# A hybrid decoder step on one core: attention output built transposed, experts drained behind their loop, pairs of expert rows added on TensorE

## The chip, the core and the metric

The kernel runs on one core of a Trainium2 chip. The metric is the device time of one execution in microseconds (us). Matrix products run on TensorE (PE; PEld is its weight load), elementwise work on VectorE (DVE), ScalarE (ACT) and GpSimd (POOL). SP issues most transfers; ACT and POOL issue some. Engines meet at counting semaphores: `.then_inc(s, 1)` counts up, `wait_ge(s, n)` holds the engine's queue until the count is there. Each engine works through its own list in order.

## The reference, cut to what matters

2048 prompt tokens and 8 x 4 sample tokens (2080 rows of 1024) go through one layer.

```python
u, v_a, q, k, v_b, gates = split(h @ w_in)            # h = modulated rms_norm(x)
out_a = gelu(u) * (tril(w_s) @ layer_norm(gelu(v_a)) + b_s)   # chunks of 128 tokens, 4 groups
p = sink_softmax(rope(q) @ rope(k).T)                 # 8 heads of 64, 2 key/value heads, window 128
out_b = p @ v_b
x1 = x + gate1 * ((g_a * (out_a @ w_pa) + g_b * (out_b @ w_pb)) @ w_o)
# each row of h2 goes to 2 of 32 experts, in blocks of 128 rows of one expert
yb = (silu(xb @ w_gate[e]) * (xb @ w_up[e])) @ w_down[e]
y  = rms_norm(x1 + gate2 * (weight_0 * yb_0 + weight_1 * yb_1)) * normf_g
```

Everything is f32. Most large products are made of three products of a high and a low part in fp32r (`three`, L254); the others are plain f32 products.

## The kernel before, in words

Six stages follow each other, each with its own block of engine programs and a barrier of all engines between: `condition`, `sweep_mixers` (to about 620 us), `sweep_gate_a`, `sweep_gate_b` with the router, `list_blocks` and `experts` (about 1558 to 2146 us), `combine` (to the end).

**sweep_mixers** goes over 16 tiles of 128 tokens and one of 32 (the sample). The attention's second half runs one tile late. On PE, `tile(i)` (L856) runs: q projection, k and v projection, the 16 transposes of the probabilities of tile i-1 (after `probs`, ACT's last exponential), v projection of mixer A, the products of probabilities and values of tile i-1 (L887: 16 of 128 x 64, into rows of tokens), transposes of q and k, two of eight steps of the u projection, four transposes of `out_b`, the other six steps, the spatial mixing (L918). Then follow the transposes of the next h, the scores (L928) and the transposes of `out_a`. DVE's `tile` (L753) runs: rotary of q, `sums` (L727, the reciprocal 1/z), rotary of k, `back_probs` (L738: half of the turned probabilities out of PSUM; ACT copies the other half), `norm_v` with `out_b` in its midst (L744: the result times 1/z, out of PSUM), `low_b`, the norm of the next tile, `out_a`, `low`, softmax. The output of the attention is kept as high and low parts of its transpose (`obT`) and stored for the next stage.

**sweep_gate_a** starts by loading and splitting 16 slices of 128 weight rows (w_in's gate, w_pa, w_pb) through four buffers.

**list_blocks** works out which block of 128 rows belongs to which expert and stores the fields of each block, with the ring slot of the expert's weights, and the number of blocks.

**experts** has a ring of four weight slots, filled by SP. Step b does, on PE: transposes of hidden rows b-1, gate and up products of block b, transposes of gathered rows b+1, down products of b-1 (L2081). ACT's step (L1969): hidden rows b-1, tanh of b, high part of the gathered rows b+1, high part of the weights of b+2 (L1942, two halves), the weighing of the output of b-1 (L1958), records. POOL's step: gather b+2, scatter b-1 (L1883). The loops run steps in pairs up to the next even number at or above the number of blocks, so that step b makes the output of block b-1.

**combine** goes over the 17 tiles again: DVE adds the two expert rows of each token (L2206), multiplies by gate 2 (L2208), adds x1 (L2211) and, after ACT's sum of squares and POOL's root, scales to the final norm (L2215). Pairs are loaded by ACT's queue (L2174), x1 and the gates by SP's, four tiles ahead. DVE starts after all three gate rows have landed.

## Time and profile before

| | us |
|---|---|
| median of 3 runs (2252.49 to 2255.87) | 2255.22 |
| the profiled execution | 2261.7 |
| its span, first to last instruction | 2260.1 |
| PE busy | 1931.8 (85%) |
| DVE busy | 1094.1 (48%) |
| ACT busy | 759.3 (34%) |
| POOL busy | 269.8 (12%) |

A busy time is a sum over the whole span, and the stages have different limits; so a stretch says more than the sum. In a timeline each row gives start and duration, the engine, the line, the operation with output and inputs, how many instructions were merged (x8), and in brackets how long the engine was idle before it and which work ended that. A plain f32 product shows as two PE records, a transpose as one. The granted clock of TensorE is 1.00 at 2.4 GHz and 0.50 at 1.2 GHz.

### The profile page before, as it was taken

To read this page: it belongs to the slowest core of one execution; us is meant where nothing else is said; L and a number is where in the kernel's file an instruction comes from. 1 tells how busy PE (TensorE), PEld (TensorE's weight loads), DVE (VectorE), ACT (ScalarE), POOL (GpSimd) and SP (SyncE) were. 2 spreads that over 40 slices of the span, in tenths; PEclk is the share of its full clock that TensorE was granted. 3 is DMA by queue.
4 is the path that set the end of the run, shared out by engine and by line. 5 is a ranking of instruction groups with operands and counts; after the bars stand their busy time and mean duration, and the time that the engine had idled before them with its cause. 6 is when DMAs were issued, how large, how long until landed. Compare 5 with 4: busy or idle time off the path is not lost. (4 is left out here: it accounts for less than half of the span.)

```text
span 2260.1 us, 30494 instructions
## 1 busy us (share of the span) xinstructions
PE 1931.8 (85%) x9577; PEld 1502.8 (66%) x9578; DVE 1094.1 (48%) x1912; ACT 759.3 (34%) x1323; POOL 269.8 (12%) x334
## 2 busy tenths in 40 slices
PE   6699999999869999996599999991799999999600
PEld 2588888888647777773488888860566666666400
DVE  3466666666330000012355555553566666666558
ACT  2244444444130000002212112110466666666512
POOL 0000000000000000000000101001122222222213
PEclk9799999999779999998799999995799999999855
DMA  8321222222084454534544433412987454999187
GB/s 282 122 87 74 87 86 95 95 94 78 22 307 182 178 193 166 205 112 171 180 149 148 149 130 139 145 63 62 320 299 263 162 192 141 310 306 307 35 334 290
DMA packets 196410, 381.98 MB, mean 169 GB/s; under 512 B 46174, under 2 KB 125534, under 8 KB 190178
## 3 DMA queue, kind: packets, MB, share of 16 engines
q1 hardware_dynamic: 156532, 304.92, 38.9%
q0 software_dynamic: 21936, 59.40, 7.0%
q10 hardware_dynamic: 17904, 17.19, 2.5%
q8 instruction: 20, 0.33, 0.1%
q14 instruction: 18, 0.15, 0.0%
HBM read 297.10 MB, written 104.26 MB: 178 GB/s over the span
## 5 line engine op out<-in xcount | busy, mean ns | idle before, releaser
L2011 DVE TENSOR_TENSOR gate_up_lo<-expert_ring,gate_up_hi 128x2048 fp32r<-128x2048 f32 x106 | 238.2, 2289 | 162.3 <-ACT gate_up_hi L1942 162.3
L1942 ACT CAST gate_up_hi<-expert_ring 128x2048 fp32r x106 | 196.6, 1902 | 159.8 <-issue 122.0
L260 PE MATMUL mix<-w_mix_hi,hT_hi 128*128 128x512 f32 (+3 forms) x544 | 203.8, 375 | 3.8 <-DVE hT_lo L640 2.6
L262 PE MATMUL mix<-w_mix_lo,hT_hi 128*128 128x512 f32 (+3 forms) x544 | 198.7, 365 | 0.0
L261 PE MATMUL mix<-w_mix_hi,hT_lo 128*128 128x512 f32 (+3 forms) x544 | 198.4, 365 | 0.0
L2081 PE MATMUL ex<-expert_ring,hidden_T 128*128 x400 | 181.8, 597 | 8.8 <-issue 8.6
L1150 DVE SCALAR_TENSOR_TENSOR ma_rows<-tanh_rows,ga 128x512 f32<-128x512 f32 (+1 forms) x34 | 21.8, 683 | 340.5 <-PE ga L262 190.1
L260 PE MATMUL ex<-gate_up_hi,gathered_T_hi 128*128 128x512 f32 x408 | 165.4, 405 | 6.1 <-DVE gathered_T_lo L2002 6.1
L262 PE MATMUL ex<-gate_up_lo,gathered_T_hi 128*128 128x512 f32 x408 | 161.0, 394 | 0.0
L261 PE MATMUL ex<-gate_up_hi,gathered_T_lo 128*128 128x512 f32 x408 | 160.5, 393 | 0.0
L260 PE MATMUL gb<-w_b_hi,h_parts_b 128*128 128x512 f32 (+1 forms) x272 | 109.7, 403 | 28.7 <-DVE w_b_lo L1449 18.9
L2081 PEld LDWEIGHTS ex<-expert_ring,hidden_T 128*128 128x128 f32 x400 | 72.0, 190 | 84.9 <-issue 84.8
L1883 POOL DMA_INDIRECT weighted_rows<-y_block,row_records x50 | 81.9, 1638 | 382.4 <-ACT y_block L1958 382.4
L260 PE MATMUL ga<-w_a_hi,h_parts 128*128 128x512 f32 (+1 forms) x272 | 110.0, 404 | 19.2 <-DVE w_a_lo L1135 14.4
L260 PEld LDWEIGHTS mix<-w_mix_hi,hT_hi 128*128 128x128 f32 (+1 forms) x544 | 100.7, 185 | 23.8 <-issue 7.3
L262 PEld LDWEIGHTS mix<-w_mix_lo,hT_hi 128*128 128x128 f32 (+1 forms) x544 | 100.5, 185 | 18.5
L261 PEld LDWEIGHTS mix<-w_mix_hi,hT_lo 128*128 128x128 f32 (+1 forms) x544 | 100.8, 185 | 16.5
L260 PE MATMUL ga<-w_a_hi,mixer_parts 128*128 128x512 f32 (+1 forms) x272 | 106.3, 391 | 3.0 <-DVE w_a_lo L1135 2.9
L260 PE MATMUL gb<-w_b_hi,merged_T_hi 128*128 128x512 f32 (+1 forms) x272 | 107.5, 395 | 1.1 <-ACT merged_T_hi L1397 1.1
L261 PE MATMUL ga<-w_a_hi,h_parts 128*128 128x512 f32 (+1 forms) x272 | 107.9, 397 | 0.0
L261 PE MATMUL gb<-w_b_hi,h_parts_b 128*128 128x512 f32 (+1 forms) x272 | 107.7, 396 | 0.0
L262 PE MATMUL ga<-w_a_lo,h_parts 128*128 128x512 f32 (+1 forms) x272 | 107.6, 396 | 0.0
(295 smaller groups left out, 3813.4 us busy)
## 6 DMA issues: line engine op xcount, KB each, us to landing
expert_ring<-in_w_gate SPq DMA_DIRECT2D x32, 1024.0 KB, 6.1
expert_ring<-in_w_up SPq DMA_DIRECT2D x32, 1024.0 KB, 8.6
expert_ring<-in_w_down SPq DMA_DIRECT2D x32, 1024.0 KB, 10.3
h_parts<-hT_split SPq DMA_DIRECT2D x16, 1024.0 KB
mixer_parts<-oT_split SPq DMA_DIRECT2D x32, 512.0 KB
w_ada_part<-in_w_ada SPq DMA_DIRECT2D x16, 1024.0 KB, 10.7
h_parts_b<-hT_split SPq DMA_DIRECT2D x16, 1024.0 KB
expert_pairs<-weighted_rows ACTq DMA_DIRECT2D x16, 1024.0 KB, 8.0
```

Source lines behind the costliest of these rows:

```text
L260: nc_mm(out, left[0], right[0], start=first, stop=False)
L261: nc_mm(out, left[1], right[0], start=False, stop=False)
L262: return nc_mm(out, left[0], right[1], start=False, stop=last)
L1150: last = nc.vector.scalar_tensor_tensor(out=ma[0:m, par, at], in0=tg[0:m, at], scalar=1.0, in1=ps[2 + n][0:m, :], op0=ALU.add, op1=ALU.mult)
L1883: pool.indirect_dma_start(out=s["y2"], out_offset=bass.IndirectOffsetOnAxis(ap=rec[:, slot, 0:1].bitcast(U32), axis=0), in_=y[:, slot % 2, ...
L1942: nc.scalar.copy(wg[par][0][:, n * HG:(n + 1) * HG], w[:, bass.ds(slot * GU + n * HG, HG)]).then_inc(w_hi, 1)
L2011: nc.vector.tensor_tensor(wg[par][1][:, at], w[:, bass.ds(slot * GU + n * HG, HG)], wg[par][0][:, at].bitcast(F32), ALU.subtract).then_inc ...
L2081: last = nc.tensor.matmul(ps[5 + n][:, :], hT[par][:, k, :], w[:, bass.ds(at, 512)], start=(k == 0), stop=(k == 1))
```

## The change

It has six parts.

1. In the mixers the probabilities are multiplied by 1/z before they are turned (`weighed`); values are the stationary operand and four heads' turned probabilities the moving one, so that four products give the transposed output at once, one key/value head in each half of the partitions. The four transposes of `out_b` go. PE turns the probabilities behind the v projection and makes the products amid the u projection; DVE copies its half of them inside `norm_v`, and norms the next tile before `low_b`; on ACT the gelu of v goes ahead of the copy of probabilities, and `keep_v` goes behind `back_out`.
2. The output's rows now stand in another order, so `w_pb` is loaded in that order, each slice in two transfers of 64 rows.
3. `list_blocks` stores a fifth field, half of the number of blocks less one; two more small DVE steps.
4. The experts' loops end one step earlier; the last block's down product, weighing and scatter come behind the loop, with a record slot of their own. ACT weighs between the two halves of the weights' cast.
5. SP loads x1 of tiles 0 to 7 and the three gate rows into ring slots 0, 2 and 1 once their last expert's weights are split. The ring is kept for `combine`.
6. In `combine` PE adds the two expert rows by products with the identity into PSUM, and DVE multiplies by the gate from there. Its loops are written out.

```diff
+                nc.vector.tensor_tensor(sc[:, :, :], sc[:, :, :], tiny[:, 48:56].unsqueeze(2).to_broadcast([P, NH, 2 * P]),
+                                        ALU.mult).then_inc(weighed, 1)
...
-            def out_b(i):
-                dve.wait_ge(pv_done, i + 1)
-                nc.vector.tensor_tensor(ob[:, :].rearrange("p (h d) -> p h d", d=HD), ps[4][:, :].rearrange("p (h d) -> p h d", d=HD),
-                                        tiny[:, 48:56].unsqueeze(2).to_broadcast([P, NH, HD]), ALU.mult).then_inc(ob_ready, 1)
-
             def low_b(i):
                 dve.wait_ge(obT_hi, i + 1)
-                nc.vector.tensor_tensor(obT[:, 1, :], ps[5][:, :], obT[:, 0, :].bitcast(F32), ALU.subtract).then_inc(obT_lo, 1)
+                nc.vector.tensor_tensor(obT[:, 1, :], ps[4][:, :], obT[:, 0, :].bitcast(F32), ALU.subtract).then_inc(obT_lo, 1)
...
                     sums(i - 1)
                 keys(i, P, c)
-                if not first:
-                    back_probs(i - 1)
-                norm_v(i, P, c, None if first else lambda: out_b(i - 1))
+                norm_v(i, P, c, None if first else lambda: back_probs(i - 1))
+                norm(i + 1, m_next, g_next)
                 if not first:
                     low_b(i - 1)
-                norm(i + 1, m_next, g_next)
                 out_a(i, P, bs)
                 low(i + 1, m_next)
                 softmax(i, mask_i, 0)
...
-                    pe.wait_ge(probs, i)
+                pe.wait_ge(q_parts, i + 1)
+                project(3, AW, 512, m).then_inc(v_done, 1)
+
+                if not first:
+                    pe.wait_ge(weighed, i)
                     for h in range(NH):
                         for j in range(2):
                             t = 2 * h + j
                             last = turn(ps[4 + t // 4][:, (t % 4) * P:(t % 4 + 1) * P], sc[:, h, j * P:(j + 1) * P])
                     last.then_inc(p_turned, 1)
-
-                pe.wait_ge(q_parts, i + 1)
-                project(3, AW, 512, m).then_inc(v_done, 1)
-
-                if not first:
-                    pe.wait_ge(pT_a, i)
-                    pe.wait_ge(pT_d, i)
-                    pe.wait_ge(v_moved, i * 2)
-                    for h in range(NH):
-                        g = h // NC
-                        for j in range(2):
-                            last = nc.tensor.matmul(ps[4][:, h * HD:(h + 1) * HD], pT[:, 2 * h + j, :],
-                                                    vv[:, j, g * HD:(g + 1) * HD], start=(j == 0), stop=(j == 1))
-                    last.then_inc(pv_done, 1)
...
-                project(2, 0, 512, m, range(0, 2))
-                if not first:
-                    pe.wait_ge(ob_ready, i)
-                    for k in range(4):
-                        last = turn(ps[5][:, k * P:(k + 1) * P], ob[:, k * P:(k + 1) * P])
-                    last.then_inc(ob_turned, 1)
-                project(2, 0, 512, m, range(2, KD)).then_inc(u_done, 1)
+                project(2, 0, 512, m, range(0, 4))
+                if not first:
+                    pe.wait_ge(pT_a, i)
+                    pe.wait_ge(pT_d, i)
+                    pe.wait_ge(v_moved, i * 2)
+                    for j in range(2):
+                        for g in range(NKV):
+                            heads = pT[:, 2 * NC * g:2 * NC * (g + 1), :].rearrange("p (h j) q -> p h j q", j=2)[:, :, j, :]
+                            last = nc.tensor.matmul(ps[4][g * HD:(g + 1) * HD, :].rearrange("p (h q) -> p h q", h=NC),
+                                                    vv[:, j, g * HD:(g + 1) * HD], heads, start=(j == 0), stop=(j == 1))
+                    last.then_inc(pv_done, 1)
+                project(2, 0, 512, m, range(4, KD)).then_inc(u_done, 1)
...
+            for c in range(NC):
+                sp.wait_ge(raw_lo, KD + 4 + c - 3)
+                for g in range(NKV):
+                    h = g * NC + c
+                    sp.dma_start(raw[c][g * HD:(g + 1) * HD], a["w_pb"][0, h * HD:(h + 1) * HD, :]).then_inc(raw_in[c], 16)
...
+def late_rows(ring):
+
+    slot = lambda n: ring[:, n * GU:(n + 1) * GU].rearrange("p (k d) -> p k d", d=D)
+    gates = [slot(1)[:, k, :] for k in range(3)]
+    return (lambda at, m: slot(2 * (at % 8 // 4))[0:m, at % 4, :]), gates
...
+            x1, gates = late_rows(w)
+            for n, e in ((0, NE - 4), (1, NE - 2)):
+                wait_apart(sp, w_lo, last_block(e) * 2, passed)
+                for k in range(4):
+                    at = 4 * n + k
+                    sp.dma_start(x1(at, P), s["x1"][at * P:(at + 1) * P, :]).then_inc(x1_in, 16)
+                if n == 0:
+                    wait_apart(sp, w_lo, last_block(NE - 3) * 2, passed)
+                    sp.dma_start(gates[0], s["ada"][0:1, GATE2 * D:].to_broadcast([P, D])).then_inc(gates_in, 16)
+                    sp.dma_start(gates[1][0:MS, :], s["ada"][1:1 + DEC_B, GATE2 * D:].unsqueeze(1)
+                                 .to_broadcast([DEC_B, DEC_T, D])).then_inc(gates_in, 16)
+                    sp.dma_start(gates[2], a["normf_g"].unsqueeze(0).to_broadcast([P, D])).then_inc(gates_in, 16)
+            sp.wait_ge(gates_in, 48)
+            sp.wait_ge(x1_in, 128)
...
+            rest = listed(pool, 4, 0)
+            scatter(rest * 2 + 1, LAST)
+            wait_apart(pool, stored[0], rest * 16 + 16, passed)
+            wait_apart(pool, stored[1], rest * 16 + 16, passed)
...
-                weights(b + 2, par)
+                weights(b + 2, par, (0,))
                 weigh(b - 1, (slot - 1) % 4, landed, before)
+                weights(b + 2, par, (1,))
...
-            step(4, 0, 16, 16)
             with act.Fori(1, QUADS) as q:
                 with act.If(q * 4 < total):
+                    step(q * 4, 0, q * 16, q * 32 - 16)
                     step(q * 4 + 1, 1, q * 16 + 16, q * 32)
+                with act.If(q * 4 + 2 < total):
                     step(q * 4 + 2, 2, q * 16 + 16, q * 32)
-                with act.If(q * 4 + 2 < total):
                     step(q * 4 + 3, 3, q * 16 + 16, q * 32 + 16)
-                    step(q * 4 + 4, 0, q * 16 + 16, q * 32 + 16)
-            ran = (total + 1) // 2 * 2
+            rest = listed(act, 4, 0)
+            records(rest * 2 + 1, LAST)
+            hidden(rest * 2 + 1, 1)
+            weigh(rest * 2 + 1, LAST, 16, rest * 16)
...
+            rest = listed(pe, 4, 0)
+            turn_h(rest * 2 + 1, 1)
+            out(rest * 2 + 1, 1)
...
+            def load(i, m):
+                sp.wait_ge(summed, i - NX + 1)
+                sp.dma_start(x(i, m), s["x1"][i * P:i * P + m, :]).then_inc(x_in[i % NX], 16)
...
+                dve.wait_ge(paired, i + 1)
+                for h in range(2):
+                    at = slice(h * 512, (h + 1) * 512)
+                    last = nc.vector.tensor_tensor(o[0:m, k, at], ps[2 * k + h][0:m, :], gate[0:m, at], ALU.mult)
+                last.then_inc(weighted, 1)
+                if i >= NX:
+                    dve.wait_ge(x_in[i % NX], i // NX * 16)
+                dve.wait_ge(weighted, i + 1)
+                nc.vector.tensor_tensor(o[0:m, k, :], o[0:m, k, :], x(i, m), ALU.add).then_inc(summed, 1)
...
+        @block.tensor
+        def _(pe):
+            ident = kept["ident"]
+
+            def tile(i, m):
+                k = i % NB
+                pe.wait_ge(g_in[k], i // NB * 16 + 16)
+                if i >= NB:
+                    pe.wait_ge(weighted, i - NB + 1)
+                for h in range(2):
+                    for n in range(2):
+                        last = nc.tensor.matmul(ps[2 * k + h][0:m, :], ident[0:m, 0:m], g[0:m, k, n, h * 512:(h + 1) * 512],
+                                                start=(n == 0), stop=(n == 1))
+                last.then_inc(paired, 1)
```

## Rows read from the trace of the kernel before

**Rows 1.** The page: length of the profiled execution.
```profile
span 2260.1 us, 30494 instructions
```
**Rows 2.** Busy time in stretches: start:end, length, each engine's us, PEclk, DMA share, GB/s.
```profile
300.00:400.00 100.00, 99.47 (x627) 86.66 (x626) 62.13 (x126) 43.89 (x110) 5.35 (x14) 1.00 0.21 81
...
1800.00:1900.00 100.00, 98.03 (x408) 67.84 (x407) 64.75 (x60) 63.45 (x80) 26.43 (x20) 1.00 0.50 168
...
2146.60:2167.50 20.90, 0.00 (x0) 0.00 (x0) 0.00 (x0) 0.00 (x0) 0.10 (x1) 0.50 0.89 358
2167.50:2240.00 72.50, 0.00 (x0) 0.00 (x0) 66.14 (x55) 15.81 (x27) 24.19 (x26) 0.50 0.93 350
```
**Rows 3.** Timeline of PE in one tile of the mixers: start, us, what.
```profile
306.85 0.48 PE L260 MATMUL mix<-w_mix_hi,hT_hi 128*128 128x512 f32 x1
...
333.33 3.68 PE L887 MATMUL mix<-v_prev_cur_next,probs_T 128*128 128x64 f32 x32
336.85 0.61 PE L839 MATMUL mix<-identity,q_rotated 128*128 128x128 f32 x4
...
337.32 0.48 PE L260 MATMUL mix<-w_mix_hi,hT_hi 128*128 128x512 f32 x1
...
338.79 0.60 PE L839 MATMUL mix<-identity,out_b_rows 128*128 128x128 f32 x4
339.14 0.48 PE L260 MATMUL mix<-w_mix_hi,hT_hi 128*128 128x512 f32 x1
```
**Rows 4.** Timeline of PE: products in two row groups, and in four column groups.
```profile
345.20 2.00 PE L928 MATMUL mix<-kT_prev_cur,qT 64*128 64x256 f32 x16
...
809.18 1.05 PE L1206 MATMUL ga<-w_ada_part,c_now 128*9 128x512 f32 x8
```
**Rows 5.** Timeline of DVE and ACT in the same tile of the mixers.
```profile
326.43 0.20 DVE L734 RECIPROCAL tiny<-tiny 128x8 f32<-128x8 f32 x1
...
328.29 1.28 DVE L741 COPY probs_T<-mix 128x512 f32<-128x512 f32 x2
...
336.36 0.55 DVE L681 TENSOR_SCALAR v_rows<-v_rows,ln_stats,tiny 128x512 f32<-128x512 f32 x1 [1.17 <-POOL tiny L479]
...
333.53 0.60 ACT L549 ACTIVATE v_rows<-mix 128x512 f32<-128x512 f32 x1 [3.10 <-PE mix L262]
```
**Rows 6.** The page's costliest groups: count, busy us, mean ns, idle time before.
```profile
L2011 DVE TENSOR_TENSOR gate_up_lo<-expert_ring,gate_up_hi 128x2048 fp32r<-128x2048 f32 x106 | 238.2, 2289 | 162.3 <-ACT gate_up_hi L1942 162.3
```
**Rows 7.** The experts' steps, by line (count, ns, first and last start); then timelines.
```profile
L2069 PE MATMUL ex<-identity,hidden x100: 272/273/476, 1609.3 to 2118.7; 128*128 128x128 f32 x100
...
2117.87 3.71 ACT L1942 CAST gate_up_hi<-expert_ring 128x2048 fp32r x2 [1.44 <-issue]
...
2121.48 1.25 ACT L1958 ACTIVATE y_block<-ex,row_records 128x512 f32<-128x512 f32 x2
...
2131.75 1.26 ACT L1958 ACTIVATE y_block<-ex,row_records 128x512 f32<-128x512 f32 x2
...
2125.17 3.60 PE L2081 MATMUL ex<-expert_ring,hidden_T 128*128 x8
```
**Rows 8.** The end of the experts' stage by line: duration in ns, start.
```profile
L1772 POOLq DRAIN  x1: 8479/8479/8479, 2137.3 to 2137.3; - x1
```
**Rows 9.** Groups of DVE in the last stage: busy us, mean ns, idle before.
```profile
L2215 DVE SCALAR_TENSOR_TENSOR out_rows<-out_rows,rms_c,normf 128x1024 f32<-128x1024 f32 (+1 forms) x17 | 21.7, 1277 | 1.5 <-POOL rms_c L2163 1.5
...
L2206 DVE TENSOR_TENSOR out_rows<-expert_pairs 128x1024 f32<-128x1024 f32 (+1 forms) x17 | 20.7, 1220 | 37.5 <-DMA gate_sample<-ada_rows 32.9 <-DMA out<-out_rows 4.6
```
**Rows 10.** Busy time in stretches where the clock is low or has risen.
```profile
597.50:600.00 2.50, 2.50 (x17) 2.13 (x17) 0.00 (x0) 0.00 (x0) 0.00 (x0) 0.50 0.00 0
635.00:640.00 5.00, 4.91 (x12) 3.89 (x13) 4.05 (x4) 3.14 (x3) 0.00 (x0) 0.50 0.88 281
640.00:645.00 5.00, 5.00 (x22) 4.08 (x21) 3.55 (x4) 3.15 (x3) 0.00 (x0) 0.92 0.89 327
...
1066.00:1072.00 6.00, 4.54 (x18) 2.80 (x16) 3.23 (x3) 3.15 (x3) 0.00 (x0) 1.00 0.97 359
```

More of the change, by code:

```diff
@@ L591, in tile @@
                     back_out(i - 1)
+                keep_v(i, first)
                 gelu_u(i, P, first)
@@ L1035, in slices @@
                 yield a["w_pa"][0, k * P:(k + 1) * P, :]
-            for k in range(4):
-                yield a["w_pb"][0, k * P:(k + 1) * P, :]
         @block.sync
@@ L1954, in weigh @@
                 if before is not None:
-                    act.wait_ge(stored[slot % 2], before)
+                    act.wait_ge(stored[half(slot)], before)
                 act.wait_ge(rec_in[slot], landed)
                 for n in range(2):
-                    last = nc.scalar.activation(y[:, slot % 2, n * 512:(n + 1) * 512], ps[5 + n][:, :], ACT.Copy, scale=weight(slot))
+                    last = nc.scalar.activation(y[:, half(slot), n * 512:(n + 1) * 512], ps[5 + n][:, :], ACT.Copy, scale=weight(slot))
                 last.then_inc(y_out, 1)
@@ L2216, in norm @@
                                                op0=ALU.mult, op1=ALU.mult).then_inc(done, 1)
-            add(0, 0, P, mods, 0, True)
-            for k in range(1, NB):
-                add(k, k, P, mods, 0, True)
-                norm(k - 1, k - 1, P)
-            with dve.Fori(1, GROUPS) as p:
-                for k in range(NB):
-                    add(p * NB + k, k, P, mods, p)
-                    norm(p * NB + k - 1, (k - 1) % NB, P)
+            for i in range(NT):
+                add(i, i % NB, P, mods, i // NB, i < NB)
+                if i:
+                    norm(i - 1, (i - 1) % NB, P)
             add(NT, 0, MS, mods_s, GROUPS)
@@ L2228, in _ @@
             norm(NT, 0, MS)
+        @block.tensor
[11 more added lines that the diff above has]
+                last.then_inc(paired, 1)
+            for i in range(NT):
+                tile(i, P)
+            tile(NT, MS)
 _INS = ["x_prompt", "x_sample", "cache_k", "cache_v", "c_prompt", "c_sample", "w_ada", "b_ada", "norm1_g", "w_in", "ln_v_g",
```

126 lines of the change are left out of this document (52 added, 74 removed).

## The prediction

> **What bounds the kernel now.** I read the page first, then the busy time by stretches. The span is 2260.1 us [rows 1], the profiled execution 2261.7 us, 6.5 us above the median of the runs shown (2255.22 us); sums are made against 2261.7. The stretches split the kernel in two. In the sweep of the mixers (300 to 400 us) and in the experts (1800 to 1900 us) PE has no idle time to speak of, at a granted clock of 1.00; from 2146.6 us on, in the last stage, PE does nothing, DMA is at 0.89 to 0.93, and DVE works 66 of 72.5 us [rows 2]. So in the first two stages an edit is worth what it takes from PE, provided that nothing comes late for PE. In the last one DVE and DMA share the bound, and both must get less.
>
> **The sweep of the mixers.** One tile takes 30.47 us, from one start of the u projection to the next (306.85 to 337.32). The products of probabilities and values take 3.52 us of PE (333.33 to 336.85: 16 products, 32 records), and the four transposes of their result 0.35 us (338.79 to 339.14) [rows 3]. The change replaces both by four products of 128 x 512 and no transposes. An f32 product of that size costs two records 0.43 us apart, 0.86 us: L2081 has 8 records in 3.60 us [rows 7]. In series the four would take 3.45 us, and the change would gain 0.4 us a tile. But the two key/value heads write partitions 0 to 63 and 64 to 127, two halves of the array's columns. The nearest row is L1206: four products of 128 x 512 in four column groups, 8 records in 1.05 us. L928 alternates two row groups: 16 records of 256 columns in 2.00 us (1.92 to the next work), where 3.4 would be serial [rows 4]. I take 2.0 us for the new four (1.75 for perfect overlap, 3.45 for none).
>
> The trace shows no weight load beside L1206 that lengthens it, though all its products use the full 128 rows. The Trainium skill says the reverse of such a case (TensorE: Matmul & The Clock Gate, Part 3, "What overlaps and what doesn't"): weight loads overlap matmuls in flight only when the row group differs. By that rule eight loads of 64 columns would show, an estimate of 1.1 us a tile, and the total would be some 17 us above mine; here the row decides.
>
> Is anything late for PE? The scaling by 1/z moves from 512 columns of the result (0.69 us) to all 2048 of the probabilities. A DVE operation of 128 x 2048 takes 2.29 us [rows 6]. It starts behind the reciprocal, 326.43 + 0.20 us, and ends at 329.0; the keys behind it end at 330.0. PE now does the v projection first (325.8 to 331.4, 5.55 us as before), so the scaled rows are there 2.4 us early, and the rotated keys 3 us before their transposes (333.1). The 0.25 us that PE waited for the exponentials goes. The next to come late is the copy of the turned probabilities. The v projection now ends 1.96 us earlier; the gelu, 333.53 before, moves to 331.57; normalising v (L681, 336.36 before) to 334.4; DVE's copy of 1.28 us then ends at 336.4 [rows 5]. PE is through the transposes and four of eight steps of u at 336.4: a dead heat, for which I charge 0.1 us. Behind that copy DVE has the last two steps of v (1.4 us) and the norm of the next tile (2.5 us), done at 340.3; PE wants the latter at 342.1. The low part of the output ends at 341.0, the scores want it at 343. The end of the tile (high and low part of h, then q) keeps its distance. New period: 30.47 - 3.52 - 0.35 - 0.25 + 2.0 + 0.1 = 28.4 us, so 2.0 us saved in each of 15 tiles and some 1.5 in the sample's tile: **31.5 us** (7 with serial products, 36 with full overlap).
>
> **Loading w_pb in halves, two more steps in the list.** Four more issues on SP of 0.35 us at most, partly under conversions; two DVE steps of about 0.2 us and a quarter more of a tiny store. Together **+1 us** (0 to 3).
>
> **The experts.** One step is 10.0 us where nothing is late. There are 50 (L2069: 100 records, two a step), 509.3 us from first to last, mean 10.39 [rows 7]; 19 us lie in hiccups, the long first step included. The change runs 49 steps and puts the 50th's product behind the loop. That doesn't save a whole step: PE has the last hidden rows turned at 2118.97, but ACT reaches them only behind its casts and the weighing. Before, ACT casts from 2117.87 and weighs from 2121.48; after, it casts a half (1.9), weighs (1.25), casts the other (1.85) and copies the hidden rows at about 2123. Their product needs 3.6 us at full clock and 6.9 at half (PE has then stood for 4.4 us), and the weighing 1.3: done between 2128.3 and 2131.8, before at 2133.0 [rows 7]. I take **3 us**. Weighing 1.85 us earlier in all steps lets the scatter, and the gather queued behind it on POOL, go earlier; DVE's second half of the cast comes 1.2 us later, with 4 us to spare. Of the 19 us I give it **4** (0 to 12). The drain of POOL at the stage's end, 8.48 us, stays [rows 8]. Late loads (4.2 MB of x1, 1.1 MB of gates, 13 us at 0.4 MB/us) start when the last down weights have been asked for, near 2092 us; they are in by about 2107, with the stage ending near 2131, so they cost nothing unless they hold up a gather: up to 13 us, if they delayed every step they touch.
>
> **The last stage.** Now it lasts 113.5 us (2146.6 to 2260.1): 20.9 us until DVE starts, as seven large loads and the gates all land first, then 17 tiles. DVE does three operations of 1.22 us and one of 1.28 [rows 9], 4.95 a tile. After: the scaling reads PSUM in two halves (1.28, as the copy that DVE makes in the mixers [rows 5]), then 1.22 and 1.28: 3.8 us. PE does four f32 products a tile: 3.45 us at full clock, 6.9 at half. The bytes fall from 35.2 MB (17.0 of pairs, 8.5 of x1, 8.5 of stores, 1.2 of gates) to 29.8 (x1 of nine tiles, no gates). The rate at full DMA share is 358 / 0.89 to 350 / 0.93, 0.38 to 0.40 MB/us [rows 2]. The first pair lands about 4.7 us after the start (1.05 MB, 2 us under way); PE begins at half clock. In the load stage it worked from 635.1 us and the stretch to 640 is at 0.50, the next at 0.92 [rows 10], so I charge the first tile 5.9 us; DVE starts near 10.8. DVE alone would end at 10.8 + 16 x 3.8 + 10.2 = 82 us, with 10.2 us for the last tile through square, roots, norm and store as now. DMA asks for more: until the last pair lands, 21.3 MB of reads and 12 stores, 27.6 MB, at 0.39 are 71 us; + 2 + 3.5 (PE) + 10.2 = 87 us. I take 87, a gain of **26.5 us** (19 to 31).
>
> **Sum.** 2261.7 - 31.5 + 1 - 3 - 4 - 26.5 = 2197.7; less the 6.5 us to the median, 2191.
>
> **Rivals.**
> (a) *The column halves run in series.* For: the loads of two halves share the rows. Against: L1206. The sweep gains 7 us: 2216.
> (b) *PE stays at half clock in the last stage.* PE works in bursts between DMA waits; with small products the clock stayed at 0.50 through 597.5 to 600 with PE busy all the time. Against: with PE busy 4.54 of 6 us the clock was 1.00 [rows 10], and a cold PE works without a break. Each tile then takes 6.9 us: 5 + 17 x 6.9 + 8 = 130 us for the stage, 43 more: 2234. [...]
> (c) *Slower than before.* The moving operand now jumps from head to head (runs of 128 columns, 256 apart). Were it read at half rate and in series, the four products would cost 6.9 us, 3.0 a tile more than what they replace: the sweep loses 45 us where I have it gain 31.5: 2268. It decides from 5.9 us a tile on. No row has such an operand at 512 columns; nothing in the rows speaks for it.
> (d) *Late loads hold up the experts*, so the transfers have only moved: 13 us back, 2204.
> (e) *The hiccups of the experts go, and the overlap is full*: 12 and 36 us: 2179.
>
> **How the numbers follow.** Mine 0.68, its own range 2181 to 2203; (a) 0.12, (b) 0.06, (c) 0.03, (d) 0.05, (e) 0.06. The range 2174 to 2220 leaves out (b), (c) and the tails. About 0.2% is what a measurement of this kernel tells from no change. Faster 0.95, within 0.2% 0.01, slower 0.04.
>
> **What would show it.** The tile's period at 28.4 us and the new products at 2.0; no wait for the scaled rows, at most 0.3 for the copies. 49 steps of about 10.3 us. DVE in the last stage starting 11 us after its first load, 4.3 to 5 us a tile, clock 1.00 from the second tile. Wrong if the period is above 29, if the clock in the last stage is 0.50, or if POOL's drain grows.

## The result, and the profile after

The changed kernel takes 2189.18 us (median of 4 runs, 2186.97 to 2190.69); the kernel before took 2255.55 us beside it (4 runs, 2252.49 to 2258.23). The ratio is 0.9705, with a 95% interval of 0.9689 to 0.9722. The forecast was 2191 us, from 2174 to 2220. Two executions further below took about twice as long as all others (4534.72 us of the kernel with VectorE's additions, 4081.90 us of the one with three edits together) and are left out, so the medians of these two kernels are of three runs.

The page of the changed kernel begins:

```profile
span 2189.0 us, 29834 instructions
```

Its execution took 2190.69 us, so the sums below are made on spans: 2260.1 [rows 1] to 2189.0, 71.1 us less. Where each stage starts shows where they came from. Each marker is the start of the stage's first load or memset.

| stretch of the span | before | after | difference |
|---|---|---|---|
| up to the end of the sweep of the mixers | 626.5 | 592.5 | -34.0 |
| first gate stage | 420.5 | 418.7 | -1.8 |
| second gate stage | 511.0 | 510.9 | -0.1 |
| list of blocks and experts | 588.7 | 573.1 | -15.6 |
| last stage | 113.4 | 93.8 | -19.6 |

Busy time by stretches of the changed kernel, with the columns of [rows 2]. The first two rows answer to the first two there, the other three are the last stage: until DVE's first operation, until TensorE's last burst, and the end.

```profile
300.00:400.00 100.00, 99.62 (x574) 80.72 (x572) 76.34 (x147) 51.56 (x131) 10.25 (x13) 1.00 0.27 103
1800.00:1900.00 100.00, 99.84 (x420) 69.96 (x419) 65.54 (x60) 65.87 (x80) 38.40 (x20) 1.00 0.63 217
2095.20:2107.60 12.40, 6.21 (x9) 2.75 (x10) 0.01 (x1) 0.00 (x0) 0.09 (x1) 0.55 0.88 338
2107.60:2172.00 64.40, 54.35 (x113) 21.55 (x112) 50.38 (x55) 16.09 (x28) 9.61 (x26) 0.95 0.94 364
2172.00:2189.00 17.00, 7.37 (x16) 1.90 (x14) 12.20 (x13) 3.47 (x7) 2.93 (x8) 0.68 0.34 134
```

In the experts, PE goes from 98.03 us in 100 to 99.84: the small gaps have gone. In the last stage DVE now works 50 of 64 us, where it worked 66 of 72.5 [rows 2]; DMA is at 0.94 (before 0.93), and the clock at 0.95.

Timeline of PE in a tile of the mixers, as [rows 3]:

```profile
300.70 2.00 PE L913 MATMUL mix<-kT_prev_cur,qT 64*128 64x256 f32 x16
...
317.28 1.91 PE L830 MATMUL mix<-identity,scores 128*128 128x128 f32 x16
...
322.42 1.94 PE L893 MATMUL mix<-probs_T,v_prev_cur_next 128*64 128x512 f32 x8
324.29 0.50 PE L260 MATMUL mix<-w_mix_hi,hT_hi 128*128 128x512 f32 x1
...
329.05 2.00 PE L913 MATMUL mix<-kT_prev_cur,qT 64*128 64x256 f32 x16
```

The scores of two neighbouring tiles start 28.35 us apart (before 30.47). The new products hold PE for 1.87 us (322.42 to 324.29), and no row before the turning of the probabilities shows a wait.

The 50 pairs of records that turn the hidden rows, as in [rows 7], take 497.6 us from first to last, where as many took 509.4:

```profile
L2090 PE MATMUL ex<-identity,hidden x100: 272/273/475, 1571.8 to 2069.4; 128*128 128x128 f32 x100
```

PE in the last stage. Each row is one stretch of products without a wait, eight records a tile:

```profile
2101.39 19.90 PE L2250 MATMUL c<-expert_pairs,identity 128*128 128x512 f32 x40 [20.54 <-DMA expert_pairs<-weighted_rows]
...
2135.68 9.17 PE L2250 MATMUL c<-expert_pairs,identity 128*128 128x512 f32 x16 [2.31 <-DMA expert_pairs<-weighted_rows]
...
2149.86 3.70 PE L2250 MATMUL c<-expert_pairs,identity 128*128 128x512 f32 x8 [0.20 <-DMA expert_pairs<-weighted_rows]
...
2161.34 5.21 PE L2250 MATMUL c<-expert_pairs,identity 128*128 128x512 f32 x8 [2.75 <-DMA expert_pairs<-weighted_rows]
...
2171.54 7.83 PE L2250 MATMUL c<-expert_pairs,identity 128*128 128x512 f32 x16 [1.04 <-DMA expert_pairs<-weighted_rows]
```

A tile costs 3.70 us at full clock. Behind the waits of 2.31 and 2.75 us it is dearer (5.21 us for one, 9.17 for two), behind those of 0.20 to 1.34 us it isn't; the last row is slow only in its last records, from 2177.8 us on. The length of the wait alone doesn't decide it: with the same last stage, the kernel with the products head by head has a tile of 5.40 us behind a wait of 1.99, and the one with the early turning a tile of 3.70 us behind a wait of 2.72.

### The profile page after: what moved, and what is told of

It reads as the page before. It is cut to its first block and busy times, and to the rows that moved or that the text cites. A ratio compares the mean times of both kernels' runs of the same rounds, so it can differ in the third digit from the quotient of the medians.

```text
span 2189.0 us, 29834 instructions
## 1 busy us (share of the span) xinstructions
PE 1959.1 (90%) x9233; PEld 1468.1 (67%) x9234; DVE 1093.0 (50%) x1906; ACT 753.0 (34%) x1318; POOL 326.0 (15%) x333
## 5 line engine op out<-in xcount | busy, mean ns | idle before, releaser
L1893 POOL DMA_INDIRECT gathered<-h_rows,row_tokens x52 | 133.2, 2562 | 56.2 <-issue 38.2
L262 PEld LDWEIGHTS mix<-w_mix_lo,hT_hi 128*128 128x128 f32 (+1 forms) x544 | 100.6, 185 | 19.2
L261 PEld LDWEIGHTS mix<-w_mix_hi,hT_lo 128*128 128x128 f32 (+1 forms) x544 | 100.9, 185 | 16.4
L262 PE MATMUL gb<-w_b_lo,h_parts_b 128*128 128x512 f32 (+1 forms) x272 | 107.5, 395 | 0.0
## 6 DMA issues: line engine op xcount, KB each, us to landing
expert_ring<-in_w_down SPq DMA_DIRECT2D x32, 1024.0 KB, 12.6
```

What stands on the lines that cost most here:

```text
L261: nc_mm(out, left[1], right[0], start=False, stop=False)
L262: return nc_mm(out, left[0], right[1], start=False, stop=last)
L1893: pool.indirect_dma_start(out=xg[:, slot % 2, :], out_offset=None, in_=s["h2"], in_offset=bass.IndirectOffsetOnAxis(ap=idx[:, slot, 0:1].b ...
```

## The experiments

Nearly all are one edit of the changed kernel (once of the kernel before), each timed against the kernel before in three rounds. The medians are read against 2189.2 us. The median of the kernel before was 2255.6 us with the first result, and 2258.4, 2258.1 and 2257.7 us on the three chips used here, so differences under some 3 us are read from the profile or not at all.

### The mixers: why four products take 1.9 us, and what the new order is worth

**Both products of one head, then both of the other.** In the changed kernel the heads alternate.

```
-                    for j in range(2):
-                        for g in range(NKV):
+                    for g in range(NKV):
+                        for j in range(2):
```

> The changed kernel with the four products of probabilities and values of a mixers' tile in another order: first both of key-value head 0, then both of head 1, instead of the two heads alternately. Side by side theory (two neighbouring products of 64 output rows each, in different halves of the array, run at the same time, which is why the four take 1.9 us and not 3.6): only the middle two can still pair, so the four take about 2.8 us, +0.9 us in each of some 16 tiles whose period TensorE sets, +14 us on 2189. Rival (a product with 64 output rows simply costs about half of one with 128, whatever stands beside it): 1.9 us again and no change within 4 us.

Measured: 2189.07 us (ratio 0.9694, 0.9668 to 0.9720), no change. The timeline of PE in that kernel:

```profile
324.01 1.95 PE L893 MATMUL mix<-probs_T,v_prev_cur_next 128*64 128x512 f32 x8
325.88 0.50 PE L260 MATMUL mix<-w_mix_hi,hT_hi 128*128 128x512 f32 x1
```

By what was expected this spoke for the rival, a narrow product that is cheap by itself. The next run was made to decide it.

**Both heads into the same half of the array's columns.**

```
-                            last = nc.tensor.matmul(ps[4][g * HD:(g + 1) * HD, :].rearrange("p (h q) -> p h q", h=NC),
+                            last = nc.tensor.matmul(ps[4 + g][0:HD, :].rearrange("p (h q) -> p h q", h=NC),
```

> The changed kernel with the products of probabilities and values of both key-value heads written to rows 0 to 63, that of head 1 in another bank; head 1's half of the attention output is therefore not what the reference computes. All else (four products of 128 x 512, 64 output rows, the strided operand) stays. Side by side theory: two products in the same half of the columns can't run together; the four take 3.5 us where they take 1.9, +1.6 us in each of 16 tiles, +25 us on 2189. Rival, which the run with another order of the four speaks for: a product of 64 output rows costs half by itself, 1.9 us again, no change within 4 us.

Measured: 2217.11 us (0.9816, 0.9794 to 0.9838), 28 us more. PE's timeline there:

```profile
334.96 3.65 PE L893 MATMUL mix<-probs_T,v_prev_cur_next 128*64 128x512 f32 x8
338.54 0.50 PE L260 MATMUL mix<-w_mix_hi,hT_hi 128*128 128x512 f32 x1
```

3.58 us instead of 1.87. The sweep ends at 620.1 us, 27.6 later than in the changed kernel. So the overlap is real and needs two halves; the narrow shape alone gives nothing. Both runs together say more than either theory: two products in the same half, issued one behind the other, don't keep those of the other half from running beside them. My +14 us for the other order took the issue order for the order in which they run, and that was wrong.

**The probabilities turned ahead of the v projection, as before.**

```
+                if not first:
+                    pe.wait_ge(weighed, i)
...
+                    last.then_inc(p_turned, 1)
+
                 pe.wait_ge(q_parts, i + 1)
                 project(3, AW, 512, m).then_inc(v_done, 1)
-
-                if not first:
-                    pe.wait_ge(weighed, i)
...
-                    last.then_inc(p_turned, 1)
```

> The changed kernel with the probabilities turned ahead of the v projection, where the kernel before has them, still after VectorE's scaling. Theory that the new place is what hides the scaling: in the changed kernel TensorE comes to the v projection at 311.8 us of the profile and VectorE's scaled scores end at 314.9 us, so TensorE stands 3.1 us a tile, 15 to 16 times: +45 to +50 us, most of the 34 us that the mixers gained is lost and more. Rival (the period is set by VectorE or by the softmax's chain and TensorE only waits elsewhere instead): under +10 us.

Measured: 2297.12 us (1.0168, 1.0139 to 1.0198), 108 us more than the changed kernel and slower than the kernel before. The expected wait is there, and two more things with it. PE's timeline:

```profile
308.38 1.94 PE L893 MATMUL mix<-probs_T,v_prev_cur_next 128*64 128x512 f32 x8 [1.55 <-DVE probs_T L742]
...
329.26 3.28 PE L830 MATMUL mix<-identity,scores 128*128 128x128 f32 x16 [3.04 <-DVE scores L736]
...
342.88 1.94 PE L893 MATMUL mix<-probs_T,v_prev_cur_next 128*64 128x512 f32 x8 [1.56 <-DVE probs_T L742]
```

One tile takes 34.50 us (308.38 to 342.88), 6.15 more than 28.35. The wait is 3.04 us. Behind it PE is slow: the same 16 transposes take 3.28 us and not 1.91, 1.4 more, and the granted clock from 329 to 334 us is 0.70. The v projection is later by both, and DVE's copy of the turned probabilities, which stands behind the norm of v in DVE's order, comes 1.56 us late for the products. 3.04 + 1.37 + 1.56 = 5.97 of the 6.15. I had counted the first alone. The sweep as a whole grew by 107.6 us (its end at 700.1 instead of 592.5). Sixteen times 6.15 is 98: the tile shown is one of the shorter ones, the median of the 15 periods is 34.83 us and four of them are 35.7 to 36.1, and what lengthens those is open.

### The experts: where 16 us went

**ScalarE's weighing put back behind both halves of the cast.**

```
                 weights(b + 2, par, (0,))
-                weigh(b - 1, (slot - 1) % 4, landed, before)
                 weights(b + 2, par, (1,))
+                weigh(b - 1, (slot - 1) % 4, landed, before)
```

> The changed kernel with ScalarE's weighing of the block before put back behind both halves of the cast of the weights. Theory A (the gaps of 0.4 to 0.6 us that TensorE had ahead of the down products, 8.6 us in all in the kernel before, are waits for that weighing, which holds the banks): they come back, with VectorE's and the gather's small waits, +9 to +13 us. Rival B (the gaps came from the body of the loops, which begins with an even step now): no change within 3 us.

Measured: 2204.9 us (0.9756, 0.9728 to 0.9785), 15.7 us more.

**The kernel before, with the weighing between the halves and nothing else.** The edit is the reverse of the one above, made in the kernel before.

> The kernel before with one edit: ScalarE weighs the block before between the two halves of the cast of the weights. Theory A: the 13.6 us that 49 experts' steps gained come with this edit alone, so -9 to -13 us on 2255.5, gaps ahead of the down products near 1 us. Rival B (loop bodies or late loads did it): no change within 3 us, and gaps of 8 to 9 us still there.

Measured: 2239.7 us (0.9921, 0.9896 to 0.9945), 18.7 us less than the kernel before on the same chip (2258.4). One moved call explains the experts' gain and a little more. The lengths of the 49 steps between the turned hidden rows, read from PE's timeline, show how even it makes them:

| kernel | first step | median | steps over 10.2 us, without the first and last | their excess over 10 us |
|---|---|---|---|---|
| before | 12.6 | 10.01 | 18 | 16.4 |
| before, weighing moved | 13.7 | 10.01 | 0 | 0 |
| changed | 13.2 | 10.01 | 3 | 2.2 |
| changed, weighing back | 13.3 | 10.01 | 16 | 15.8 |

But theory A named the wrong wait. In the kernel before, the gap ahead of the down products isn't a wait for the weighing. It follows the gather. First PE's weight loads, then PE, in one long step of the kernel before:

```profile
1782.03 0.86 PEld L2050 LDWEIGHTS ex<-identity,gathered 128*128 128x128 f32 x8 [0.68 <-DMA gathered<-h_rows,row_tokens]
```
```profile
1783.81 3.70 PE L2081 MATMUL ex<-expert_ring,hidden_T 128*128 x8 [0.69 <-issue]
```

There are eight late gathers of this kind from 1600 to 2060 us, and each has a gap of 0.64 to 0.70 us ahead of the down products 1.7 to 1.8 us later. Eight smaller gaps (0.31 to 0.53) have no late gather ahead of them, but nearly one: in the four of them for which the trace has the landing, the gather landed 0.32 to 0.41 us ahead of the turning, and where it landed 0.90 us ahead or more there is no gap. The weighing, for which theory A had PE wait, had ended 1.6 us or more before the down products in all sixteen. The down products need two entries of the block list, which PE reads behind the turning of the gathered rows in its order. I read a gap as those reads with nothing left to hide them, once the sequencer has stood at the gather; that the gap is made of these reads is argued from the order of the code, no run took them away. What is shown is the cause ahead of it. The gather stands in POOL's order behind the scatter, and the scatter waits for the weighing. Counted from the turned hidden rows (medians of 46 steps), the moved call brings the weighing forward from 3.2 to 1.1 us, the scatter from 5.4 to 3.3 and the gather from 7.4 to 4.8. The gathered rows are turned 5.5 us into the next step, so the gather has 8.1 us before and 10.6 us after. It needs 7.6 us to land in the median and up to 8.9 before, 8.1 and up to 9.6 with the weighing moved; with the longer lead none is late. The lines of the gather, in the kernel before and in the one with the weighing moved:

```profile
L1877 POOL DMA_INDIRECT gathered<-h_rows,row_tokens x44: 998/1004/2556, 1604.6 to 2064.9; - x44
...
  PEld ex L2050: 4.4, 8
...
DMA to landing us min/median/max: 3.4/7.6/8.9
```
```profile
L1877 POOL DMA_INDIRECT gathered<-h_rows,row_tokens x46: 2292/2654/2663, 1602.6 to 2066.1; - x46
...
DMA to landing us min/median/max: 4.8/8.1/9.6
```

The same two views show POOL's gather itself going from 1.00 to 2.65 us, of which more at the end.

**50 steps and no part behind the loop.** It is compared with the kernel told below that has the late loads in the last stage, because the 50th step reads a slot that they fill.

```
             step(3, 3, 16, 16)
+            step(4, 0, 16, 16)
             with act.Fori(1, QUADS) as q:
                 with act.If(q * 4 < total):
-                    step(q * 4, 0, q * 16, q * 32 - 16)
                     step(q * 4 + 1, 1, q * 16 + 16, q * 32)
+                    step(q * 4 + 2, 2, q * 16 + 16, q * 32)
...
-            rest = listed(act, 4, 0)
-            records(rest * 2 + 1, LAST)
-            hidden(rest * 2 + 1, 1)
-            weigh(rest * 2 + 1, LAST, 16, rest * 16)
```

> The kernel with the late loads in the last stage (2201.7 us) and, besides, the experts' loops of the kernel before: 50 steps, the last one's three-part products thrown away, and no part behind the loop. Theory A (the new end gave back in ScalarE's list reads and the cold product what it saved in the dropped step): the same as that kernel, within 3 us. Rival B (my forecast of 3 us saved): 2204 to 2206.

Measured: 2197.86 us (0.9728, 0.9702 to 0.9753), against 2201.74 for the kernel that differs in this alone: 3.9 us less, on another chip and with intervals that overlap, so the times alone don't show it. The profiles agree in sign. From the first turned hidden rows to the first request of the last stage it takes 520.4 us, and 522.8 in the kernel with the new end. The seven kernels of this study that have the new end and the weighing in its new place, without the further edits of that end described below, take 522.1 to 523.9; the two with the old end and that weighing take 519.6 and 520.4. The new end costs 2 to 4 us where I had it save 3. That holds with the weighing in its new place: with the weighing behind both halves, the old end takes 537.4 us over the same stretch (the kernel before) and the new one 537.3.

**The number of the last pair read early.**

```
             weights(2, 0)
             total = listed(act, 3, 0)
+            rest = listed(act, 4, 0)
+            records(rest * 2 + 1, LAST)
...
-            rest = listed(act, 4, 0)
-            records(rest * 2 + 1, LAST)
             hidden(rest * 2 + 1, 1)
```

(and the same read on TensorE's side)

> The changed kernel with the number of the last pair read, and the last block's records asked for, before the loops (both are known there), so that ScalarE goes from its last step straight to the hidden rows, and TensorE to their transposes. Theory A (the tail of the experts gave nothing because ScalarE read lists and issued a DMA for 3.3 us ahead of the hidden rows, and TensorE read one for 1.8 us and had gone cold, 5.6 us for a product of 3.6): -4 us, -3 to -6. Rival B (the end of the stage is set by the scatter and POOL's drain, whenever the product comes): no change within 1 us.

Measured: 2187.32 us (0.9689, 0.9669 to 0.9708), 1.9 us less. The end of the experts in the changed kernel, ACT and PE in one timeline, and POOL's drain by line:

```profile
2069.28 0.43 PE L2090 MATMUL ex<-identity,hidden 128*128 128x128 f32 x2 [1.83 <-issue]
...
2069.51 1.89 ACT L1961 CAST gate_up_hi<-expert_ring 128x2048 fp32r x1
...
2074.68 0.38 ACT L1969 ACTIVATE hidden_T<-ex 128x256 f32<-128x256 f32 x1 [3.28 <-issue]
...
2075.28 5.57 PE L2102 MATMUL ex<-expert_ring,hidden_T 128*128 x8 [5.57 <-ACT hidden_T L1969]
...
2081.02 1.26 ACT L1977 ACTIVATE y_block<-ex,row_records 128x512 f32<-128x512 f32 x2 [5.96 <-PE ex L2102]
...
2083.20 0.98 POOL L1899 DMA_INDIRECT weighted_rows<-y_block,row_records  x1 [11.44 <-ACT y_block L1977]
...
2095.24 2.67 ACTq L2187 DMA_DIRECT2D expert_pairs<-weighted_rows  x4
```
```profile
L1769 POOLq DRAIN  x1: 8400/8400/8400, 2085.9 to 2085.9; - x1
```

And with the number read early:

```profile
2072.13 0.38 ACT L1969 ACTIVATE hidden_T<-ex 128x256 f32<-128x256 f32 x1 [1.02 <-issue]
...
2072.73 5.24 PE L2102 MATMUL ex<-expert_ring,hidden_T 128*128 x8 [3.88 <-ACT hidden_T L1969]
```

ACT's idle time ahead of the hidden rows falls from 3.28 to 1.02 us, and from the product of the block before to the first request of the last stage it is 28.8 us instead of 31.4. The product itself stays slow, 5.24 us, because PE has still stood for 3.88 us. So ScalarE's reads held 2.3 us, and the cold product another 1.6 to 2.0 of its 3.6.

### The last stage: the loads or the additions

**The first eight tiles of x1 and the gates loaded in the last stage, as before.**

```
+            for at in range(NX):
+                sp.dma_start(x(at, P), s["x1"][at * P:(at + 1) * P, :]).then_inc(x_in[at], 16)
+                if at == 0:
+                    sp.dma_start(mods, s["ada"][0:1, GATE2 * D:].to_broadcast([P, D])).then_inc(const_in, 16)
+                    sp.dma_start(gf, a["normf_g"].unsqueeze(0).to_broadcast([P, D])).then_inc(const_in, 16)
...
```

(and the same loads out of the end of the experts)

> The changed kernel with the first eight tiles of x1 and the gates loaded in the last stage, ahead of its other loads as before, and TensorE's additions kept. Theory A (the last stage is set by DMA, so what moved out of it is what it gained): 5.3 MB more at 0.4 MB/us, +13 us, +11 to +17. Rival B (VectorE's fourth operation was the gain, the loads were hidden anyway): under +4 us.

Measured: 2201.74 us (0.9747, 0.9723 to 0.9770), 12.6 us more. DVE starts 21.5 us after the first request, much as before the change (20.9).

**The pairs added by VectorE, as before.**

```
-                dve.wait_ge(paired, i + 1)
-                for h in range(2):
-                    at = slice(h * 512, (h + 1) * 512)
-                    last = nc.vector.tensor_tensor(o[0:m, k, at], ps[2 * k + h][0:m, :], gate[0:m, at], ALU.mult)
-                last.then_inc(weighted, 1)
+                dve.wait_ge(g_in[k], n * 16 + 16)
+                nc.vector.tensor_tensor(o[0:m, k, :], g[0:m, k, 0, :], g[0:m, k, 1, :], ALU.add).then_inc(weighted, 1)
+                dve.wait_ge(weighted, i * 2 + 1)
+                nc.vector.tensor_tensor(o[0:m, k, :], o[0:m, k, :], gate[0:m, :], ALU.mult).then_inc(weighted, 1)
```

> The changed kernel with the two expert rows added by VectorE as before (four operations, 4.95 us a tile, TensorE unused in the last stage); the early loads kept. Theory A (DMA sets the stage): VectorE would end at 6.2 + 16 x 4.95 + 10.2 = 96 us where the stage takes 93.8, so it becomes the bound by little: +2 to +6 us. Rival B (the identity products were the larger part of the gain of 19.6 us): +10 us or more.

Measured: 2192.8 us (0.9713, 0.9688 to 0.9738), 3.6 us more, on a chip on which the kernel before was 2.6 us slower too; the last stage is 93.3 us, against 93.8 in the changed kernel's profile and 89.8 to 94.4 in five others with the same last stage. So the additions by identity products, which the title names, are worth at most some 4 us of 66, and these runs don't tell that from nothing. The rows of this kernel show why; DVE's first operation, and busy time in the stretches that answer to those of the changed kernel:

```profile
2102.33 1.23 DVE L2217 TENSOR_TENSOR out_rows<-expert_pairs 128x1024 f32<-128x1024 f32 x1 [27.06 <-DMA expert_pairs<-weighted_rows]
```
```profile
2107.60:2172.00 64.40, 0.00 (x0) 0.00 (x0) 62.62 (x53) 14.94 (x26) 33.42 (x28) 0.50 0.95 376
2172.00:2190.10 18.10, 0.00 (x0) 0.00 (x0) 13.71 (x12) 3.45 (x6) 6.55 (x7) 0.50 0.25 99
```

DVE has 4.95 us of work a tile and is busy 62.6 of 64.4 us: it is the bound, by little. But it starts 5.5 us after the first request, and behind TensorE 12.4 us, because the first tile's four products run at half clock for 6.2 us. What the products save a tile (1.1 us) they pay for with this start, and with DVE's waits for its stores (12.7 us in nine waits in the changed kernel).

**Pairs asked for behind TensorE's addition.**

```
-            for k in range(NB):
-                tile(k, k, P, k == 0)
-                pairs(NB + k, k, P)
...
+            for i in range(NT + 1):
+                m = P if i < NT else MS
+                if i + NB <= NT:
+                    act.wait_ge(paired, i + 1)
+                    pairs(i + NB, i % NB, P if i + NB < NT else MS)
+                tile(i, i % NB, m, i == 0)
```

> The changed kernel with ScalarE asking for the pair of rows of tile i+4 as soon as TensorE has added tile i, ahead of the squares of tile i and no more behind them. Theory A (DMA stands still at the start of the last stage, at a share of 0.67 to 0.86 from 6 to 25 us, because the next pair is asked for only behind VectorE and ScalarE): -3 us, -2 to -5. Rival B (DMA is full in the middle of the stage and the end is a chain behind the last pair, so earlier requests only queue): no change within 1 us.

Measured: 2189.43 us (0.9693, 0.9670 to 0.9717), no change. The last burst of products comes 68.1 us after the first request instead of 76.3, at 2167.40 in its profile; the stage ends 22.9 us behind it instead of 17.5. From 2162.6 us on DVE waits for nothing but 1.1 us of the last root. It is behind by then, having stood 10.5 us in seven waits for its own stores to land. The reads come sooner, the stores and DVE's work don't, and the stage ends at nearly the same time.

**The first four pairs loaded beside POOL's drain.**

```
+            for par in range(2):
+                wait_apart(act, stored[par], rest * 16 + 16, passed)
+            for k in range(4):
+                act.dma_start(first_pairs(w)[:, k, :, :], s["y2"][k * 2 * P:(k + 1) * 2 * P, :]
+                              .rearrange("(t k) d -> t k d", k=2)).then_inc(pairs_in, 16)
+            act.wait_ge(pairs_in, 64)
```

> The changed kernel with the first four pairs of rows loaded at the end of the experts' stage by ScalarE, as soon as the last scatter has landed, into the place of the down weights, while POOL drains. Theory A (the 12 us from the last scatter to the last stage hold 9 us in which DMA does nothing, and DMA sets the last stage): four loads of 1 MB, 10.5 us at 0.4 MB/us, lie beside the drain: -7 us, -5 to -9. Rival B (the drain waits for the queues too and ends only when the loads have): under -2 us.

Measured: 2189.22 us (0.9689, 0.9664 to 0.9714), no change. Rival B has the number, but its reason is wrong: the drain doesn't wait for the loads. The drains of POOL and of ACT by line, and busy time in two stretches:

```profile
L1774 POOLq DRAIN  x1: 8400/8400/8400, 2088.9 to 2088.9; - x1
L1774 ACTq DRAIN  x1: 8/8/8, 2101.3 to 2101.3; - x1
```
```profile
2090.00:2100.00 10.00, 0.00 (x0) 0.00 (x0) 0.00 (x0) 0.00 (x0) 0.00 (x0) 0.50 0.98 399
2100.00:2110.00 10.00, 7.74 (x14) 3.44 (x15) 2.00 (x3) 0.00 (x0) 0.09 (x1) 0.69 0.04 15
```

POOL's drain is not longer (8.40 us, done at 2097.3). DMA is full from 2090 to 2100 us as planned. But ACT waits for all four pairs, until 2101.3, so the stage begins 4 us later after the scatter; and the fifth pair is asked for only when the first tile is through cold TensorE, DVE and ACT, at 2110.6. The idle time of DMA has moved from ahead of the loads to behind them.

**The three together.**

> Three edits together on the changed kernel: the number of the last pair read early, pairs asked for behind TensorE's addition, and the first four pairs loaded beside POOL's drain. If each keeps its gain (2 us measured; 3 and 7 us expected): 2177, between 2173 and 2182. Rival (they overlap: all three bring the same first tile forward, and DMA takes it back): 2182 to 2186.

Measured: 2186.6 us (0.9681, 0.9651 to 0.9711), 2.6 us less than the changed kernel. It is the lowest of the study, but its interval holds the changed kernel's ratio of 0.9705, so it isn't shown to be faster. In its profile the last stage takes 83.9 us, and the time from the last turned hidden rows to that stage 28.2 us instead of 25.8. The rival's 2182 to 2186 is the nearer of the two.

## Why the prediction was right

The total was off by 2 us and the signs of the large terms were right. That it was so near is in part luck. One term was too small by 10 to 12 us (the hiccups), two were too large by 5 to 7 each (the end of the experts, whose sign was wrong, and the last stage). The stages of the two profiles add up to 71.1 us of gain where 64 were forecast; the medians fell by only 66.4, because the profiled execution of the kernel before was 6.2 us above its median and that of the changed kernel 1.5.

- **The sweep of the mixers, 31.5 us: right, 34.0.** The period is 28.35 us where 28.4 was forecast and 30.47 stood before, and the products 1.87 us for 2.0. The scaled rows are in time because of the new place of the turning: with the old place the sweep costs 107.6 us more. Rival (a) asked for 7 us of gain in the sweep; with both heads in one half, where the products do run in series, its sweep gains 6.4 us (620.1 for 626.5), so (a) had the price right and the overlap wrong. Rival (c), an operand of jumps read at half rate, is out with 1.87 us.
- **w_pb and the list, +1: no sign of it.** The first gate stage is 1.8 us shorter than before in the one pair of profiles, but it takes 418.7 to 421.8 us in the profiles of kernels with the same code there. Nothing can be said below that.
- **The experts' hiccups, "Of the 19 us I give it 4": this step failed in size.** In the steps it is 14.2 us in the changed kernel (16.4 to 2.2) and 16.4 in the kernel before with that edit alone; in time, 15.7 and 18.7. The path I named, an earlier weighing, an earlier scatter and the gather behind it, is the right one. I gave it a fifth because I hadn't set the gather's landing (7.6 us in the median, up to 8.9) against the 8.1 us until its transposes. Of the long first step nothing went.
- **The end of the experts, 3 us saved: wrong.** With the weighing moved it costs 2 to 4 us. The step that failed is "copies the hidden rows at about 2123", directly behind the cast: the reads of the list and a DMA's issue stand in front of it in ACT's order, 3.28 us, and 1.83 us of such reads on PE. From the last turned hidden rows to the last stage it is 25.8 us for 28.0 before, but that is the moved weighing (25.6 in the kernel before with that edit alone). POOL's drain stayed, 8.40 us [rows 8].
- **The late loads: hidden, as forecast.** Rival (d), 13 us back, is out; with the loads in the last stage the experts are no shorter (522.8 us against 522.1 to 523.9).
- **The last stage, 26.5 us: right in sign, 7 us too large.** It is 19.6 us, or 19.2 by the means of six profiles with the new stage (92.0) and two with the old (111.2). DVE starts at 12.4 us, not 10.8: the first pair lets PE start at 6.2 us, where I had 4.7, and PE's first tile takes another 6.2; the last burst comes at 76.3 us for 73, and the end behind it takes 17.5 us for 13.7. The sum's premise, that DMA sets the stage once DVE has less to do, is half of it. With DVE's four operations kept the stage is as long within 2 us, and with the pairs asked for earlier it is as long too. I read it as two bounds so close that taking from one alone gives nothing. What moved it was the loads: 9.4 us by profile (101.4 with them in the stage, for the 92.0), and 12.6 us by time, on a chip on which the kernel before was 2.6 us slower.
- **The clock in the last stage:** 0.95 from the first tile's end. Rival (b) is out. The Trainium skill (TensorE: Matmul & The Clock Gate, "Loop structure matters more than you think") has PE go cold where a long DMA wait stands between all matmuls. Here ten groups wait for a DMA, the first for 20.54 us and the others for 0.20 to 2.75; the trace agrees for the first and for those behind 2.31 and 2.75 us, and seven stayed at full clock from their start.
- **The column halves:** the same page of the Trainium skill, Part 3, "What overlaps and what doesn't", lets a weight load overlap products in flight only where the row groups differ, and has products start strictly in order. Four products with all 128 rows in 1.87 us, in either order of issue, with weight loads beside them, go against both in this case.

## What to carry to other kernels

Ask of each DMA that an engine waits for how far ahead of its use it is asked for, and set this against its measured landing: here a moved call of 1.3 us brought 16 us, more than the additions that gave the change its name. Where two resources stand as close as DVE and DMA in this last stage, taking from one alone may give nothing; what gained here were the loads moved into an earlier stage, for which DVE had waited too. A wait of TensorE can cost more than its length (here 3.04 us became 6.15 in a tile): count what the products behind it lose at a lower clock, and what is queued behind them.

## What the runs showed of the hardware that was not expected

**POOL's indirect DMAs stand still while VectorE works on two inputs in SBUF,** as far as the one operation of that kind in this stage shows it. Moving the weighing changed the gather from 1.00 to 2.65 us and the scatter from 1.6 to 1.2. The timeline of the kernel before with that edit:

```profile
1634.80 2.29 DVE L2014 TENSOR_TENSOR gate_up_lo<-expert_ring,gate_up_hi 128x2048 fp32r<-128x2048 f32 x1 [0.67 <-ACT gate_up_hi L1944]
1635.32 2.65 POOL L1877 DMA_INDIRECT gathered<-h_rows,row_tokens  x1 [0.30 <-issue]
```

The cast's low part ends at 1637.09, the gather at 1637.97, 0.88 us later. In the changed kernel it is 1611.38 and 1612.26. In the kernel before, the scatter was the one that met that operation: 1638.04 and 1638.92, again 0.88. A gather that meets none takes 1.00 us. So did eleven gathers of the kernel before that started while DVE made `gathered_T_lo`, which has one of its two inputs in PSUM. The standstill costs nothing here, since the earlier request outweighs it. The Trainium skill (SBUF — State Buffer, "SBUF: two separate sides" and "Who interferes with whom") describes an exclusive lock of the port pair that the two engines share, held for the whole instruction; an operation of two SBUF inputs contends by it only with a GpSimd instruction that reads SBUF, and a `tensor_tensor` is said not to have stalled DMA. These rows agree with the lock, and show it for indirect DMAs from POOL, against that last remark.

**The two halves of the columns run independently in either issue order** (1.87 us alternating, 1.87 us head by head, 3.58 us in one half).

**A wait of 3.04 us cost PE 1.37 us of clock behind it,** and the last stage shows it behind some waits. In the changed kernel those of 2.31 and 2.75 us cost clock and those of up to 1.34 us cost none, but in other runs with the same stage one of 1.99 us did and one of 2.72 us didn't.
